# Output projection with the weights moving, layer norm by row statistics, in a two-layer S5, Hyena and latent-attention encoder

## The reference

```python
mixed = jnp.sum(gates * lifted, axis=2) @ w_out[i]
ple = (p[i] @ w_ple[i]) * jax.nn.sigmoid(ple_logits)
x = layer_norm(DEEPNORM_ALPHA * x + mixed + ple, ln_g[i], ln_b[i])
```

## Time and profile before

| | us |
|---|---|
| median of 3 runs | 2877.02 (2876.92 to 2879.37) |
| profiled execution, device time | 2877.76 |
| its span in the trace | 2876.2 |
| TensorE busy with matmuls | 2709.4 (94%) |
| DVE busy | 1876.5 (65%) |
| ACT busy | 1297.3 (45%) |
| POOL busy | 108.7 (4%) |
| mean of what DMA moved | 143 GB/s |

### The profile page before, as it was taken

How to read it: one execution, slowest core, us unless ns; L and a number is a source line. 1 busy time by engine, 2 the same in 40 slices (tenths; PEclk the granted TensorE clock), 3 DMA queues, 4 the chain that set the end, 5 groups by cost and what they waited for, 6 DMA issues and landing times.

```text
span 2876.2 us, 50752 instructions
## 1 busy us (share of the span) xinstructions
PE 2709.4 (94%) x18088; PEld 2429.8 (84%) x18088; DVE 1876.5 (65%) x3312; ACT 1297.3 (45%) x2319; POOL 108.7 (4%) x202
## 2 busy tenths in 40 slices
PE   5899999989999999999869999998999999999996
PEld 5799999877987879999858999987789878799996
DVE  6878787634567766565487878786255677565655
ACT  4555555624543233453334555556255433244532
POOL 1100000000000000000021000000000000000000
PEclk9999999999999999999989999999999999999999
DMA  6444444333452334555354444442344423245552
GB/s 224 151 144 149 149 143 149 124 125 133 147 169 96 111 103 137 182 176 171 115 170 151 149 145 149 149 144 101 133 152 142 162 96 118 88 158 182 176 169 88
DMA packets 115096, 411.19 MB, mean 143 GB/s; under 512 B 15300, under 2 KB 15322, under 8 KB 114448
## 3 DMA queue, kind: packets, MB, share of 16 engines
q1 hardware_dynamic: 106704, 390.12, 40.4%
q0 software_dynamic: 8256, 19.26, 2.1%
HBM read 403.02 MB, written 6.29 MB: 142 GB/s over the span
## 4 chain that ended last, share of the span: by engine, by line
PE 87%; DVE 6%; issue 3%; ACT 2%; DMA 1%; DVEq 0%; PEldq 0%; POOLq 0%; POOL 0%; ACTq 0%; PEld 0%; SPq 0%
PE bank L1447 36%; PE bank L1475 18%; PE bank L1477 9%; PE bank L1429 5%; PE bank L1568 2%; PE bank L1545 2%; PE bank L1759 2%; PE bank L1527 2%; PE bank L1723 2%; PE bank L1746 1%; PE bank L1512 1%; PE bank L1562 1%; PE bank L1636 1%; DVE WL L380 1%; PE bank L1661 1%
## 5 line engine op out<-in xcount | busy, mean ns | idle before, releaser
L366 ACT ACTIVATE WH<-ring 128x512 fp32r<-128x512 f32 x1360 | 855.7, 631 | 1278.7 <-PE bank L1447 725.0
L380 DVE TENSOR_TENSOR WL<-ring,WH 128x512 fp32r<-128x512 f32 x848 | 574.7, 690 | 533.9 <-ACT WH L366 528.7
L1475 PE MATMUL bank<-XX,WH 128*128 128x512 f32 x2304 | 826.1, 402 | 69.3 <-DVE XX L520 46.5
L1447 PE MATMUL bank<-XX,WH 128*128 128x256 f32 x3712 | 683.3, 286 | 12.6 <-DVE WL L380 8.2
L1477 PE MATMUL bank<-XX,WL 128*128 128x256 f32 x2304 | 646.6, 281 | 0.0
L1447 PEld LDWEIGHTS bank<-XX,WH 128*128 128x128 f32 x3712 | 581.0, 192 | 30.7 <-issue 23.9
L1475 PEld LDWEIGHTS bank<-XX,WH 128*128 128x128 f32 x2304 | 438.0, 190 | 171.8 <-DVE XX L520 46.9
L1447 PE MATMUL bank<-XX,WL 128*128 128x256 f32 x1856 | 526.3, 284 | 0.0
L371 DVE TENSOR_TENSOR WL<-ring,WH 128x512 fp32r<-128x512 f32 x512 | 350.9, 688 | 141.0 <-ACT WH L366 136.9
L1477 PEld LDWEIGHTS bank<-XX,WL 128*128 128x128 f32 x2304 | 439.8, 191 | 0.0
L1447 PEld LDWEIGHTS bank<-XX,WL 128*128 128x128 f32 x1856 | 357.2, 192 | 0.0
(11 more groups left out here) (297 smaller groups left out, 3649.3 us busy)
## 6 DMA issues: line engine op xcount, KB each, us to landing
ring<-in_blocks SPq DMA_DIRECT2D x736, 512.0 KB, 3.3
ARENA<-in_bc POOLq DMA_DIRECT2D x2, 2048.0 KB, 8.4
ARENA<-in_decay POOLq DMA_DIRECT2D x8, 512.0 KB, 4.6
ARENA<-in_x SPq DMA_DIRECT2D x1, 2048.0 KB, 9.8
u_scratch<-ARENA POOLq DMA_DIRECT2D x16, 128.0 KB, 2.2
ARENA<-u_scratch POOLq DMA_DIRECT2D x64, 32.0 KB, 2.8
y_scratch<-ARENA POOLq DMA_DIRECT2D x16, 128.0 KB, 2.0
ARENA<-y_scratch POOLq DMA_DIRECT2D x64, 32.0 KB, 2.7
```

The lines of the kernel that those rows point to most:

```text
L366: nc.scalar.activation(wh[q], raw(which[0], q), ACT.Copy).then_inc(wh_ready[q], 1)
L380: vec.tensor_tensor(wl[q], raw(which[0], q), wh[q].bitcast(F32), ALU.subtract).then_inc(w_used[slot(which[0], half)], 1)
L1447: ins = mm(o, w_, x_, start=start and i == 0 and n == 0, stop=stop and i == 7 and n == 2)
L1475: ins = mm(bank[b][:, :], h, xx[:, :, k, :], start=(k == 0), stop=(k == DT - 1), skip_group_check=True)
```

## The change

The out stage now has the tokens on partitions. A tile of MIXH or MIXL (128 features by 128 tokens) is the stationary operand, and 512 columns of weights are streamed from WH or WL. Bank 2g + t holds features 512g to 512g + 511 of the tokens of half t. Before its products, each bank gets its part of the residual by four transposes of RES tiles, into which the products are then accumulated. The host lays the blocks of w_out out accordingly. The stage is written out without a hardware loop; in the last block all of bank 6 comes first, and then bank 7.

The layer norm works on the banks: BN_STATS per bank, BN_AGGR per half of the tokens, the root of ACT and a Newton step on one column, and one operation per bank that writes the normalised values to `XN` (area 41 to 56). TensorE transposes XN back, into the same banks, and ACT applies ln_g and ln_b on the way from the banks to RES. ACT copies each group of RES to XH, DVE makes XL.

The splits of block 0 of the next layer (`NEXT`) and the copies to XH and XL stand now in the tail of the layer before; for layer 0 they stand ahead of the loop. Behind the last layer `NEXT` reloads the first block of layer 0, which nothing uses. POOL waits for the four copies to XH in place of x_ready, which is gone.

```diff
@@ numbers @@
-    "out":  [8, 8, 0, 0, 1, 1, 0, 0],
+    "out":  [2, 2, 2, 2, 2, 2, 2, 2],
@@ sync @@
+            for s in range(2):
+                sp.wait_ge(w_used[s], DEPTH * HALVES // RING * 2)
+                sp.dma_start(slots[s], flat[s]).then_inc(w_loaded[s], 16)
...
             for i in range(GROUPS):
-                sp.wait_ge(x_ready, DEPTH * GROUPS + (i + 1))
+                for b in (2 * i, 2 * i + 1):
+                    sp.wait_ge(psum_free[b], read_out(DEPTH - 1, "out", b, 1))
                 sp.dma_start(group(out, i), group(RES, i)).then_inc(stored, 16)
@@ gpsimd @@
-            pool.sem_inc(x_ready, GROUPS)
...
             with pool.Fori(0, DEPTH) as layer:
-                pool.wait_ge(x_ready, layer * GROUPS + GROUPS)
+                pool.wait_ge(xh_ready, layer * GROUPS + GROUPS)
                 pool.wait_ge(rope_ready, 1)
                 pool.dma_start(PAR[:], lp[layer]).then_inc(params_loaded, 16)
                 pool.dma_start(area(49, 16), bc[layer]).then_inc(params_loaded, 16)
@@ vector, ahead of the loop (and no longer in it) @@
+            make_wl(dve, v, 0, B_AX)
+            for i in range(GROUPS):
+                dve.wait_ge(xh_ready, i + 1)
+                v.tensor_tensor(group(XL, i), group(RES, i), group(XH, i).bitcast(F32), ALU.subtract).then_inc(xl_ready, 1)
@@ vector, out stage and norm @@
-                with dve.Fori(0, 3) as turn:
-                    for j in range(4):
-                        make_wl(dve, v, layer, B_OUT + j + 1, turn, 4)
...
-                        add_out(turn, j)
...
-                full(4, "out", 0)
-                free(v.tensor_scalar(MU, bank[4][:, 0:T], 1 / D, None, ALU.mult), 4)
...
-                    v.tensor_tensor(c, c, mub, ALU.subtract).then_inc(xc_ready, 1)
...
-                    st.did(v.tensor_tensor(c, c, vab, ALU.mult)); st.wait()
-                    for m in range(4 * i, 4 * i + 4):
-                        ins = v.tensor_scalar(RESt[:, m, :], RESt[:, m, :], par("ln_g", m), par("ln_b", m), ALU.mult, ALU.add)
-                    ins.then_inc(x_ready, 1)
+                def row_stats(g, t):
+
+                    full(2 * g + t, "out", 0)
+                    st.did(v.bn_stats(stats[t][:, g * 6:(g + 1) * 6], bank[2 * g + t][:, :]))
+
+                def variance(t):
+
+                    st.wait()
+                    v.memset(tmp[t], 0.0)
+                    st.did(v.bn_aggr(moments[t], stats[t])); st.wait()
+                    v.tensor_scalar(var[t], moments[t][:, 1:2], 1e-5, None, ALU.add).then_inc(var_ready, 1)
+
+                def inv_std(t):
+
+                    dve.wait_ge(root_ready, layer * 4 + (3 + t))
+                    inv_root(var[t], root[t], tmp[t])
+
+                def normalise(g, t):
+
+                    xn = XN[:, (t * 4 + g) * CW:(t * 4 + g + 1) * CW]
+                    free(v.tensor_scalar(xn, bank[2 * g + t][:, :], moments[t][:, 0:1], var[t], ALU.subtract, ALU.mult), 2 * g + t)
+
+                def low_part(i):
+
+                    dve.wait_ge(xh_ready, layer * GROUPS + (GROUPS + i + 1))
+                    v.tensor_tensor(group(XL, i), group(RES, i), group(XH, i).bitcast(F32), ALU.subtract).then_inc(xl_ready, 1)
+
+                for n in range(15):
+                    make_wl(dve, v, layer, B_OUT + n + 1)
+                    if n in (4, 8, 12):
+                        row_stats(n // 4 - 1, 0)
+                        row_stats(n // 4 - 1, 1)
+                row_stats(3, 0)
+                variance(0)
+                inv_std(0)
+                normalise(0, 0)
+                row_stats(3, 1)
+                variance(1)
+                normalise(1, 0)
+                inv_std(1)
+                normalise(0, 1)
+                normalise(1, 1)
+                make_wl(dve, v, layer, NEXT, halves=(0,))
+                normalise(2, 0)
+                normalise(2, 1)
+                low_part(0)
+                make_wl(dve, v, layer, NEXT, halves=(1,))
+                normalise(3, 0)
+                normalise(3, 1)
+                for i in range(1, GROUPS):
+                    low_part(i)
@@ scalar @@
+            for half in range(2):
+                make_wh(act, half, 0, B_AX)
+            act.wait_ge(x_loaded, 16)
+            for i in range(GROUPS):
+                a.activation(group(XH, i), group(RES, i), ACT.Copy).then_inc(xh_ready, 1)
...
+                act.wait_ge(var_ready, layer * 2 + 1)
+                a.activation(root[0], var[0], ACT.Sqrt).then_inc(root_ready, 1)
+                for half in range(2):
+                    make_wh(act, half, layer, NEXT)
+                act.wait_ge(var_ready, layer * 2 + 2)
+                a.activation(root[1], var[1], ACT.Sqrt).then_inc(root_ready, 1)
+
+                for g in range(GROUPS):
+                    for m in range(4 * g, 4 * g + 4):
+                        b = 2 * g + m // 2 % 2
+                        full(b, "out", 1)
+                        ins = a.activation(RESt[:, m, :], bank[b][:, m % 2 * T:(m % 2 + 1) * T], ACT.Identity, bias=par("ln_b", m), scale=par("ln_g", m))
+                        if m % 2:
+                            free(ins, b)
+                    for b in (2 * g, 2 * g + 1):
+                        out_of(b, "out", 1)
+                    a.activation(group(XH, g), group(RES, g), ACT.Copy).then_inc(xh_ready, 1)
@@ tensor @@
+                def out_step(b, t, k, q):
+
+                    for n, (x_, w_) in enumerate(((mixh, wh), (mixl, wh), (mixh, wl))):
+                        ins = mm(bank[b][:, :], x_[:, k, tok[t]], w_[q], start=False, stop=(k == 15 and n == 2), skip_group_check=True)
...
+                for g in range(GROUPS):
+                    pe.wait_ge(res_ready, layer * DT + (4 * g + 4))
+                    for t in range(2):
+                        take_bank(2 * g + t, "out", 0)
+                        for i in range(4):
+                            release(mm(bank[2 * g + t][:, i * P:(i + 1) * P], RESt[:, 4 * g + i, tok[t]], ident, start=(i == 0), stop=False,
+                                       is_transpose=True, skip_group_check=True))
+                    for j in range(4) if g < 3 else range(3):
...
+                for q in range(4):
+                    out_part(B_OUT + 15, q)
+                    ins = out_step(6, 0, 12 + q, q)
+                done(ins, 6)
+                for q in range(4):
+                    ins = out_step(7, 1, 12 + q, q)
...
+                for g in range(GROUPS):
+                    for b in (2 * g, 2 * g + 1):
+                        take_bank(b, "out", 1)
+                    for m in range(4 * g, 4 * g + 4):
+                        b = 2 * g + m // 2 % 2
+                        for t in range(2):
+                            at = (m % 2 * 2 + t) * P
+                            ins = nc.tensor.transpose(bank[b][:, at:at + P], XN[:, t * D + m * P:t * D + (m + 1) * P], ident)
+                        if m % 2:
+                            done(ins, b)
```

More of the change, by code:

```diff
@@ L515, in add_input @@
                     free(v.tensor_tensor(by_step, by_step, bank[m % 2][:, 0:T].rearrange("p (c t) -> p t c", t=STEP), ALU.add), m % 2)
-                make_wl(dve, v, layer, B_AX)
-                for i in range(GROUPS):
-                    dve.wait_ge(xh_ready, layer * GROUPS + (i + 1))
-                    v.tensor_tensor(group(XL, i), group(RES, i), group(XH, i).bitcast(F32), ALU.subtract).then_inc(xl_ready, 1)
                 dve.wait_ge(params_loaded, layer * 32 + 32)
@@ L1098, in _ @@
-                for j in range(4):
-                    if j < 3:
-                        make_wl(dve, v, layer, B_OUT + 13 + j)
-                    add_out(3, j)
-                for b in (0, 1):
-                    out_of(b, "out", 7)
-                full(4, "out", 0)
-                free(v.tensor_scalar(MU, bank[4][:, 0:T], 1 / D, None, ALU.mult), 4)
-                out_of(4, "out", 0)
-                mub, vab = (b.unsqueeze(1).to_broadcast([P, 4, T]) for b in (MU, VA))
-                for i in range(GROUPS):
-                    c = split(group(RES, i), 4)
-                    v.tensor_tensor(c, c, mub, ALU.subtract).then_inc(xc_ready, 1)
@@ L1112, in _ @@
-                dve.wait_ge(xc_ready, layer * GROUPS + GROUPS)
-                full(5, "out", 0)
-                free(v.tensor_scalar(VA, bank[5][:, 0:T], 1 / D, 1e-5, ALU.mult, ALU.add), 5)
-                out_of(5, "out", 0)
-                inv_root(VA, ROOT, VA2, 2)
-                for i in range(GROUPS):
-                    c = split(group(RES, i), 4)
-                    st.did(v.tensor_tensor(c, c, vab, ALU.mult)); st.wait()
-                    for m in range(4 * i, 4 * i + 4):
-                        ins = v.tensor_scalar(RESt[:, m, :], RESt[:, m, :], par("ln_g", m), par("ln_b", m), ALU.mult, ALU.add)
-                    ins.then_inc(x_ready, 1)
+                        add_ple(m - 1).then_inc(res_ready, 1)
@@ L1140, in _ @@
```

(45 more changed lines are left out.)

51 lines of the change are left out of this document (34 added, 17 removed).

## The result

| | before | after |
|---|---|---|
| median of the runs (us) | 2878.19 (2876.92 to 2881.30, 4 runs) | 2844.95 (2841.32 to 2848.39, 4 runs) |
| profiled execution, its span (us) | 2877.76, 2876.2 | 2844.58, 2842.3 |

The ratio of the two is 0.9883, with a 95% interval from 0.9866 to 0.9900: faster by some 33 us, 1.2%. Forecast were 2839 us and 2832 to 2850. The range held the time; the forecast was 6 us too low. I keep the names of the prediction: U is the end of bank 6 in the last product, T the end of bank 7.

A forecast was written before the change was run, and what follows sets the result against it. The prediction took TensorE to bound the kernel, 87% of the chain. Start +4.7, out projection -7.4, boundary -18.0 and end -17.5 sum to -38.2, from 2877.76 to 2839.6, stated as 2839 us; range 2832 to 2850.

The forecast's parts named there:

- The start: Program's start: POOL waits for all four XH copies, so in_bc lands at 33.7 in place of 29.03, +4.7 us.
- Out projection: Out stage: 384 matmuls of 512 columns replace 768 of 256, with residual transposes added and loop edges gone; -3.7 us per layer.
- 347 ns a pair, less 118.6 leaves 228.5 ns: Out stage: price of a 512-column matmul, from ax-stage pairs less the old out matmul; 384 make 87.7 us.
- the Trainium skill's rule: Matmul starts N / 2.4 GHz + about 2.5 ns apart; halving their number would give 1 us per layer, not 3.4.
- The boundary: Norm between layers: in_bc lands at T + 24.85 against T + 42.8, so the next layer starts earlier; -18.0 us.
- DVE's chain is late next: Layer boundary: after in_bc lands, DVE's chain is late next; block 1 taken up 6.3 us behind each landing.
- Block 0 hides: Layer boundary: TensorE's block 0 starts near U + 17 and is done by U + 25.5 even at half speed.
- The end: Last norm to the span's end: no parameters loaded, T + 18.5 against T + 36.0; -17.5 us.
- (a): Rival, out stage: residual transposes let the clock fall, losing 15 us with eight groups, 2854; 4 in 100.
- (b): Rival, out stage: wide matmuls back to back are slower than in pairs, at 250 ns 16.5 us, 2856; 5 in 100.
- (c): Rival, out stage: split weights streamed while ACT and DVE write the same tiles; at 300 ns, 2894; 2 in 100.
- (d): Rival, next layer: half-speed block or slower DVE chain gives back up to 8 us of boundary gain, 2847; 7 in 100.

The follow-up runs named there:

- e1: Changed kernel, but POOL's first parameter load no longer waits for the copies to XH in layer 0: 2840.29 us, ratio to before 0.9869.
- e4: Changed kernel without the residual transposes, each bank's first product starting it, so the sum lacks the residual: 2838.65 us, ratio to before 0.9854.
- e0: The changed kernel once more, unchanged, as base line for the other runs: 2845.99 us, ratio to before 0.9886.
- e6: Changed kernel, but DVE splits the next layer's block 0 after its last copy to XL, not among the normalisations: 2848.22 us, ratio to before 0.9890.
- e7: Changed kernel with earlier in_bc at start and boundary, all scalings and normalisations first, later splits, XH and XL copies at the layer's head: 2829.38 us, ratio 0.9826.
- e2: Changed kernel, but at the boundary in_bc waits only for the transposes back, and PAR, now second, for the last scaling: 2843.24 us, ratio to before 0.9877.

## Why the prediction was right, and where it was 6 us off

**The start** (+4.7): +4.9. Issue 26.13 for 26.7, 7.79 us for the transfer, and e1 shows that the moved wait is the whole of it at this place.

**Out projection** (-3.7 per layer): -2.5, 2.4 us of the miss in two layers. The step that failed is a term of the sum: "347 ns a pair, less 118.6 leaves 228.5 ns"; 233.3 ns was measured. TensorE's timeline of before shows what was wrong with the subtraction. First pairs further on, then the edge of the first loop of the out stage:

```profile
47.91 0.40 PE L1475 MATMUL bank<-XX,WH 128*128 128x512 f32 x1
...
49.68 0.40 PE L1475 MATMUL bank<-XX,WH 128*128 128x512 f32 x1
```

```profile
1341.39 0.28 PE L1447 MATMUL bank<-MIXH,WL 128*128 128x256 f32 x1
1342.59 0.38 PE L1447 MATMUL bank<-MIXH,WH 128*128 128x256 f32 x1 [0.92 <-issue]
```

The 118.6 was right for its stage: from 1318.63 to 1341.39 stand 191 intervals, the first of 0.22 us, the other 190 of 118.7 ns on average, and it is the same in all four turns. But it isn't the short matmul of the pair. In the seven pairs read the earlier trace rows the short one starts 231.5 ns behind the wide one on average, and the next wide one 115.5 ns behind the short one. The short matmul of one stage was subtracted from the pair of another, which took 3 ns too much off. And the pairs run at two paces: the five from 47.91 in 1.77 us are 354 ns each (the two parts are 236 and 117.5 in such blocks), whole blocks at the one or the other, at the same full speed. The 233.3 of the out stage lies between 231.5 and 236.

By the measured paces the matmuls go from 768 x 0.1187 = 91.1 us to 384 x 0.2333 = 89.6, so 1.5 us; the forecast had 3.4. The loop edges that went were 4.3: 1.20 - 0.12 = 1.08 at the edge shown, 1.05 and 1.06 at the other two, 0.74 ahead of the loop, and 0.1 for the slow first interval of each of the four turns. The transposes cost 3.5 (3.9 forecast), by e4. That makes 2.3 of the 2.5.

I had set the Trainium skill's rule (TensorE: Matmul & The Clock Gate, section "Wait — 56ns, not 53.3ns?") aside, because 118.6 ns did not fit N / 2.4 GHz. Neither does 233.3, 17.5 more than the rule gives. But its gain for half as many matmuls, 1 us a layer, was nearer to the measured 1.5 than my 3.4: the fixed part is 2 x 118.7 - 233.3 = 4.1 ns in these runs, between its 2.5 and the 8.7 that my figures implied. A rule that misses the level of a pace may still be near in its difference.

**The boundary** (-18.0): -16.3. ACT started at U + 7.7 (8.3 forecast) and took 2.97 a group (2.75): its four scalings 1.93, not 1.55. The 0.36 us apart was an estimate from DVE's scalings; ACT's stand 0.45 apart. The two errors nearly cancel, which is luck: the last XH copy ends at U + 19.6 (19.3). The term that was off is in_bc: 8.4 us, not 7.0, within the bounds given (in e0 and e4 it took 8.9 and 9.1, above the upper bound of 8.6). It is not made faster by the two weight loads having gone (8.6 with them). Its first packet starts 1.4 us behind its issue, where I had put 0.9 of start that no row showed; then its 2.1 MB move at 320 GB/s on average, with no weight load in flight, not at the 426 of the lower bound; and the landing is told 0.45 us behind the end of the last packet. That DVE's chain is late next, 6.3 us from landing to block 1, came out at 6.25. Block 0 hides; e6 shows that it could start 2.8 us later.

**The end** (-17.5): -16.7, T + 19.3 for T + 18.5; again ACT's scalings, 0.9 us: the last one ends at U + 19.0, 18.15 was forecast, and the store's 3.1 us follow as forecast.

**The sum**: 1.7 (boundary), 2.4 (out), 0.8 (end) and 0.2 (start) too low, less 0.75 by which the layers' insides came out faster: some 4.3 us of span. (The 0.75 is less than the 3.2 us by which the same code varied up to the out stage.) The rest of the 6 us is the time around the span (+0.7), the median above the profiled run (+0.4) and the step from 2839.6 to 2839 (0.6).

**The rivals.** (a) falls by e4: same pace without transposes, and a granted clock of 1.00 with them. The clock fell in the norm's stretch (0.77 from 1415 to 1430); before the change it had fallen at the norm's end (0.62 from 1431 to 1453, when TensorE stood still). (b) and (c) fall by the 233 ns: a wide matmul costs 4.1 ns less than two of half the columns. (d) is not seen beyond the insides' own spread.

Of the signs named for being wrong none came: 0.233 us apart is below 0.24, block 1 waits for DVE's chain, the first load moved to 26.13. Of the figures that were to show it, two were missed: the stage became 2.5 us shorter and not 3.7, and T to the end is 19.3 us and not 18 to 19.

## What to carry to other kernels

A pace that is the difference of two stages' paces was off by 4.8 ns, and that times 768 is 3.7 us; the wide matmul's own start-to-start in the same rows, 231.5 ns, would have been off by 1.8. Halving the number of matmuls at the same columns gave 1.5 us of 91; taking the norm's reductions off the path gave 16 us at each of two places. When a wait moves to the end of a loop's body, look at the first and the last turn apart: here the first paid 4.9 us for a condition it didn't need, and the last did copies and splits for a layer that didn't come. Following that list to its end (e7) gave half as much again as the change itself.

## What the runs showed that I had not expected

- A pair of 512 and 256 columns took 347 ns in 124 blocks and 353 to 354 in 14 others of one execution (blocks without a stop or a fallen clock), with the same granted clock and the same durations in the records (0.40 and 0.28 us). In the changed kernel it was so too. Which neighbour sets the pace is open; the residual transposes are not it, since the kernel before has none.
- 194 KB took 2.5 to 3.0 us to land when issued ahead of 2 MB, 7.7 to 9.7 when issued behind it on the same queue, and 5.4 and 7.9 on another queue. Putting the small load behind the big one took back part of what the earlier big one gained (e2).
- The statistics of 512 elements from a bank took 0.70 us, as long as a copy of as many (0.684), and the aggregate of 24 values 0.26.
- In e2 TensorE's block 0 started 2 us later after U than in the changed kernel (1432.83, U + 20.9), though its transposes ended at the same place; the cause is not known; whether the drain behind them does it wasn't tried.
